# Hybrid attention and recurrent layer on one core: the down projection of the ConvFFN as 2x2 blocks with seven products

## The chip, the cores and the metric

One core of a Trainium2 chip runs the whole program in one launch. The metric is the device time of that launch in microseconds, the median of several runs; lower is better. Five engines work side by side: TensorE (PE, the matrix products), VectorE (DVE), ScalarE (ACT), GpSimd (POOL) and SyncE (SP, which here issues nearly all transfers in one in-order queue). Products land in PSUM, which has eight banks; everything else stands in SBUF or in DRAM.

## The reference, cut to what matters

2048 prompt tokens and 64 sample tokens pass one layer: attention and a gated recurrence (the "mixers"), then the ConvFFN. Only the ConvFFN's end is changed.

```python
h = modulate(x, norm_ffn_g[l], shift, scale)
up, cf_new = causal_dwconv(h @ ffn_up_w[l], cf_prev, ffn_conv_w[l], ffn_conv_b[l])
val, gt = jnp.split(up, 2, axis=-1)                                   # 2 x 2816 channels
x = x + gate[:, None, :] * ((val * jax.nn.gelu(gt)) @ ffn_down_w[l])  # 2816 -> 1024: the down projection
y = rmsnorm(x, final_norm_g)
```

All arrays are float32. The kernel keeps that precision by splitting every matrix factor into two float16 halves, a high one (the value cast) and a low one (value minus high), and adding three products (high by high, high by low, low by high) for each one wanted.

## The kernel before, in words

Columns are the 2112 tokens, kept as two halves of 1056 (TH) and worked on 352 (CF) at a time. Channels are tiles of 128: 8 tiles (KT) of the model width, 22 (NF) of the hidden width.

**Up rounds.** Round f makes one value tile and one gate tile of the hidden layer. The up projection is done as 2x2 blocks with seven products (Strassen-Winograd): 7 products x 3 column blocks x 4 k-tiles x 3 passes = 252 matmuls of 352 columns. Beside it, for the tile pair of round f-1, ACT and DVE run the convolution (`first_tap`, `ffn_conv`: four DVE instructions over 2114 columns), the GeLU and the product of value and gate (`product`), and split the weights of round f+1 (`up_hi` on ACT, `up_lo` on DVE). The gated tile is split into halves too (`product_hi`, `product_lo`) and stored to DRAM (`store_hidden`).

**Down projection, before.** The eight row tiles of the down weights are loaded and split whole (`down_hi`, `down_lo`, 2816 columns each) during and after the last round. Then six column blocks c follow each other: for each of them 8 row tiles m x 22 k-tiles x 3 passes = 528 matmuls, with the hidden halves read from DRAM in one large transfer per block (`hidden`). All 3168 matmuls run through the helper `passes` (L2545), as do the products of the other stages. For each row tile DVE adds the residual (`y_new`, L2413), ACT squares it (L1628), DVE sums the squares (`add_square`), and once for each block PE sums them over the partitions (`sum_squares2`, L2767), ACT takes the root (L1620), DVE inverts it (`inverse`, L2431) and scales the tile (`finish`, L2438), and SP stores y.

**What sets the order.** Nothing is scheduled: each engine's program is written out by hand and runs in that order, and semaphores hold an instruction until what it needs is there. `pe.wait_ge(g_ev, ...)` keeps PE from a bank until DVE has emptied it.

## Time and profile before

| what | value |
|---|---|
| three timed runs | 2755.87 (median), 2757.07, 2752.3 us |
| span of the profiled execution, first to last instruction | 2749.8 us |
| so outside the span, against the median | 6.1 us |
| PE busy in the span | 2703.3 us, 98% |
| DVE, ACT, POOL busy | 1606.0 us (58%), 1301.4 us (47%), 306.4 us (11%) |
| up rounds 1 to 21 | about 1491 to 2258 us |
| down projection on PE | 2258 to 2736 us |

The profiled execution's own time is not among the three listed; its span is what the trace gives, and the time around it is taken as the difference above. A busy share of PE counts pipelined matmuls, so it says that PE has no gaps, not that it works at its peak.

### The profile page before, as it was taken

How to read it: one execution, taken by the hardware profiler on the slowest of the kernel's cores; microseconds unless marked ns; L12 is line 12 of the kernel's file. 1: busy time of each engine (PE TensorE's matmuls, PEld its weight loads, DVE VectorE, ACT ScalarE, POOL GpSimd, SP SyncE). 2: the span in 40 equal slices, each digit the busy share in tenths (PEclk: the TensorE clock that was granted, in tenths of full speed). 3: DMA queues.
4: the chain of work that ended last, by engine and by line, in shares of the span. 5: the costliest groups of instructions: out<-in, count | busy, mean ns of one | idle time of the engine just before them, and what ended most of it. 6: DMA issues, size and time to landing. Idle time of an engine off the chain costs nothing.

```text
span 2749.8 us, 49269 instructions
## 1 busy us (share of the span) xinstructions
PE 2703.3 (98%) x19058; PEld 1816.5 (66%) x19058; DVE 1606.0 (58%) x3110; ACT 1301.4 (47%) x2497; POOL 306.4 (11%) x295
## 2 busy tenths in 40 slices
PE   7999999999999999999999999999999999999998
PEld 2456666666678886559986666666666666666665
DVE  5966473746556665777787677766677663211112
ACT  4966474746566664124566445445445452211111
POOL 2600000000037896000000000000000000000000
PEclk9999999999999999999999999999999999999999
DMA  8622122121474541556641111111111165223211
GB/s 283 208 91 90 70 76 103 64 71 69 128 194 112 127 188 59 217 209 164 158 113 50 59 62 62 46 62 47 62 62 62 46 209 165 84 88 98 90 43 43
DMA packets 214342, 291.11 MB, mean 106 GB/s; under 512 B 58704, under 2 KB 163664, under 8 KB 209312
## 3 DMA queue, kind: packets, MB, share of 16 engines
q1 hardware_dynamic: 204256, 277.44, 31.8%
q10 hardware_dynamic: 8848, 8.74, 0.9%
q8 instruction: 112, 1.84, 0.3%
q0 software_dynamic: 1072, 2.65, 0.3%
q14 instruction: 54, 0.44, 0.1%
HBM read 201.96 MB, written 89.46 MB: 106 GB/s over the span
## 4 chain that ended last, share of the span: by engine, by line
PE 86%; ACT 4%; DVE 4%; DMA 3%; issue 2%; POOL 1%; SPq 0%; DVEq 0%; ACTq 0%; POOLq 0%
PE ps L2545 74%; PE ps L2637 4%; PE ps L2624 3%; PE ps L2613 2%; DMA arena<-in_w_mod_rest 2%; PE ps L2469 1%; PE ps L2651 1%; ACT arena L1288 1%; POOL arena L889 1%; PE ps L2586 1%; DVE arena L2038 1%; DVE arena L2116 1%; ACT arena L1003 1%; ACT arena L1295 1%; DMA arena<-in_w_proj 1%
## 5 line engine op out<-in xcount | busy, mean ns | idle before, releaser
L2545 PE MATMUL ps<-arena 128*128 128x352 f16 (+1 forms) x15048 | 2086.3, 300 | 5.8 <-DVE arena L2237 1.7
L2545 PEld LDWEIGHTS ps<-arena 128*128 128x128 f16 x15048 | 1410.7, 97 | 677.0 <-issue 3.4
L2413 DVE SCALAR_TENSOR_TENSOR arena<-ps,arena 128x352 f32<-128x352 f32 (+1 forms) x64 | 30.0, 490 | 353.6 <-PE ps L2545 353.6
L1446 ACT ACTIVATE arena<-ps 128x352 f32<-128x352 f32 x264 | 119.8, 464 | 190.9 <-PE ps L2545 190.9
L1628 ACT ACTIVATE arena<-arena 128x352 f32<-128x352 f32 x48 | 23.8, 496 | 377.5 <-DVE arena L2413 377.5
L2651 PE MATMUL ps<-arena 128*128 128x424 f16 (+1 forms) x960 | 173.5, 342 | 2.0 <-DVE arena L2116 1.4
L2237 DVE SCALAR_TENSOR_TENSOR arena<-arena 128x512 f16<-128x512 f32 x154 | 103.8, 689 | 120.2 <-ACT arena L1410 120.2
L2637 PE MATMUL ps<-arena 128*128 128x64 f32 (+2 forms) x1200 | 150.6, 271 | 0.5 <-DVE arena L2080 0.5
L2651 PEld LDWEIGHTS ps<-arena 128*128 128x128 f16 x960 | 92.5, 97 | 82.7 <-issue 2.4
L2637 PEld LDWEIGHTS ps<-arena 128*128 128x128 f32 (+2 forms) x1200 | 144.2, 192 | 3.1 <-issue 1.4
L1483 ACT ACTIVATE arena<-arena 128x2114 f32<-128x2114 f32 x44 | 94.6, 2149 | 101.8 <-DVE arena L2292 96.6
L1086 ACT ACTIVATE arena<-ps 128x352 f32<-128x352 f32 x192 | 80.8, 463 | 120.5 <-PE ps L2545 120.5
L2305 DVE SCALAR_TENSOR_TENSOR arena<-arena 128x2114 f32<-128x2114 f32 x44 | 106.4, 2418 | 52.3 <-ACT arena L1483 52.3
L1295 ACT ACTIVATE arena<-ps 128x512 f32<-128x512 f32 (+3 forms) x136 | 76.3, 561 | 102.5 <-PE ps L2624 102.4
L935 POOL TENSOR_TENSOR arena<-arena 128x1024 f32<-128x1024 f32 (+6 forms) x147 | 118.6, 807 | 13.8 <-POOL arena L928 3.9
L1804 DVE SCALAR_TENSOR_TENSOR arena<-arena 128x512 f16<-128x512 f32 x112 | 73.9, 687 | 64.2 <-ACT arena L1065 64.1
L2309 DVE SCALAR_TENSOR_TENSOR arena<-arena 128x2114 f32<-128x2114 f32 x44 | 106.5, 2420 | 0.4
L1288 ACT ACTIVATE arena<-arena 128x640 f32<-128x640 f32 (+5 forms) x136 | 102.8, 756 | 3.4 <-DVE arena L2059 3.2
L2059 DVE CUSTOM_DVE_ANT_0 arena<-ps,arena 128x640 f32<-128x640 f32 (+5 forms) x136 | 100.2, 737 | 0.3 <-issue 0.2
L2514 PE MATMUL ps<-arena 128*128 128x512 f16 (+1 forms) x408 | 91.6, 383 | 7.3 <-DVE arena L1734 5.3
L2624 PE MATMUL ps<-arena 128*128 128x128 f32 (+1 forms) x600 | 92.9, 281 | 5.1 <-ACT arena L1288 2.9
L1410 ACT ACTIVATE arena<-arena 128x512 f16<-128x512 f32 x154 | 93.3, 624 | 0.0
(213 smaller groups left out, 2598.2 us busy)
## 6 DMA issues: line engine op xcount, KB each, us to landing
arena<-in_w_up SPq DMA_DIRECT2D x44, 512.0 KB, 3.9
ffn_hidden<-arena SPq DMA_DIRECT2D x44, 512.0 KB, 3.3
arena<-ffn_hidden SPq DMA_DIRECT2D x5, 3872.0 KB, 16.1
arena<-gates SPq DMA_DIRECT2D x8, 2112.0 KB, 9.6
arena<-in_w_proj SPq DMA_DIRECT2D x32, 512.0 KB, 4.5
gates<-arena SPq DMA_DIRECT2D x16, 1024.0 KB, 7.6
arena<-in_w_mod_rest SPq DMA_DIRECT2D x32, 512.0 KB, 4.0
arena<-in_w_down SPq DMA_DIRECT2D x7, 1408.0 KB, 6.2
```

Of the source, the lines that this page charges most:

```text
L935: pool.tensor_tensor(out, djunk[:, :, 0:w], djunk[:, :, w:2 * w], ALU.add).then_inc(ada_step, 1)
L1288: act.activation(pr[0:x.rows, x.h, 0:x.w], pr[0:x.rows, x.h, 0:x.w], ACT.Exp, scale=-1.0, bias=least[0:x.rows, x.h:x.h + 1], accum_out=sm[ ...
L1295: act.activation(pt[:, x.h, 0:m * P], ps[:, 4, 0:m * P], ACT.Copy).then_inc(t_act, 1)
L1446: act.activation(fcp[(0, 1, 2, 0)[i]][q], ps[:, bank_of((0, 2, 3, 4)[i], q), 0:CF], ACT.Copy, scale=CSF)\
L2059: dve.tensor_tensor_reduce(pr[0:rows, h, 0:w], src, bias[x.b][0:rows, h, x.b0:x.b0 + w], 1.0, 3.0e38, ALU.add, ALU.min, least[0:rows, h:h ...
L2237: dve.scalar_tensor_tensor(fsp[:, c, :, 1, :], src.rearrange("p (k m) -> p k m", k=4), -WSF if c == 6 else WSF, fsp[:, c, :, 0, :], ALU.mu ...
L2305: dve.scalar_tensor_tensor(out, u[:, 1:1 + LF], tap(1), out, ALU.mult, ALU.add).then_inc(f_conv, 1)
L2309: dve.scalar_tensor_tensor(out, u[:, 2:2 + LF], tap(2), out, ALU.mult, ALU.add).then_inc(f_conv, 1)
L2545: mm = pe.matmul(out, wt[:, k, wp, :], act_t[:, k, hp], start=(first and k == 0 and n == 0), stop=(last and k == K - 1 and n == 2), skip_g ...
L2624: mm = pe.transpose(ps[0:k, 4 + c // 4, (c % 4) * P:(c % 4) * P + x.rows], pr[0:x.rows, x.h, c * P:c * P + k], ident[0:x.rows, 0:x.rows])
L2637: mm = pe.matmul(ps[0:x.rows, 6, 64 * x.h:64 * x.h + 64], pt[0:k, x.h, c * P:c * P + x.rows], vv[x.b][0:k, x.v0 + c, 64 * x.h:64 * x.h + 6 ...
L2651: mm = pe.matmul(out, wt[:, wp, k, :], mixT[:, k, hp, t:t + w], start=(k == k0 and m == 0), stop=(k == k1 - 1 and m == 2))
```

## The change: what it does

The down projection takes the same form as the up projection: 2x2 blocks with seven products. A block row of the weights is a pair of row tiles, a block of the inner dimension a pair of k-tiles, and the two column blocks of a product are the same 352 columns of the two token halves. So there are three groups of columns (NG), four pairs of row tiles in each, twelve steps n in all (ND), and 11 pairs of k-tiles (NI). A step has 7 products x 11 x 3 = 231 matmuls.

- The gated tile is no longer split in the up rounds (`product_hi`, `product_lo` go); SP stores it in float32.
- The sums of weight blocks are made beside the up rounds in 44 units, two in each of rounds 1 to 16 and three in each of rounds 17 to 20: SP loads a unit (256 KB), POOL forms four sums of 128x128, ACT and DVE split seven tiles into halves (`unit_hi`, `unit_lo`), SP stores them (448 KB) to DRAM. The down projection reads them from there (`weight_load`).
- For each of the three groups the 11 bases (the four blocks of gated tiles of a k-pair, 704 KB) are loaded (`base_load`), POOL forms four sums of 128x352 (`base_sums`), ACT casts three blocks and four sums (`base_hi`, 1056 and 1408 columns), DVE subtracts (`base_lo`). The float32 blocks have two stage buffers (and one more for the very first group's last base); the halves stand in one set `dact[0..10]`, shared by all groups.
- A step is cut into chunks of bases, (0,4), (4,8), (8,11): all seven products of a chunk run before the next chunk. The first step takes bases 0 to 3 together and then one at a time. The last step is one chunk.
- The seven products of a step are combined by DVE in eleven small instructions over 352 columns (two copies from PSUM by ACT).
- The sums of squares of a whole group (8 row tiles x 2 halves, 16 tiles of 352 columns) are taken on PE inside the first step of the next group.

```diff
+            def base_load(s):
+                g, i = s // NI, s % NI
...
+                    to, done = stage[s % 2], b_loaded[s % 2]
+                    if s >= 2:
+                        sp.wait_ge(b_lo, 2 * (s - 1))
+                sp.dma_start(to.rearrange("p b t -> p (b t)"),
+                             hid_d[:, g, 2 * i:2 * i + 2].rearrange("p k h t -> p (k h t)")).then_inc(done, 16)
...
+            def base_sums(s):
+                b12, b11, b22, b21 = (stage_of(s)[:, k] for k in range(4))
...
+                if s >= 2:
+                    pool.wait_ge(b_lo, 2 * (s - 1))
...
+                pool.tensor_tensor(t0, b12, b11, ALU.subtract).then_inc(b_sum, 1)
+                pool.tensor_tensor(t1, b22, b12, ALU.subtract).then_inc(b_sum, 1)
+                pool.wait_ge(b_sum, 4 * s + 1)
+                pool.tensor_tensor(t2, b22, t0, ALU.subtract).then_inc(b_sum, 1)
+                pool.wait_ge(b_sum, 4 * s + 3)
+                pool.tensor_tensor(t3, b21, t2, ALU.subtract).then_inc(b_sum, 1)
...
+            def base_hi(s):
...
+                    act.wait_ge(q_filled, pair_used(4 * g - 1, i))
+                act.activation(dact[i][:, 0:3, 0], stage_of(s)[:, 1:4], ACT.Copy).then_inc(b_hi, 1)
+                act.wait_ge(b_sum, 4 * s + 4)
+                act.activation(dact[i][:, 3:7, 0], dsum[s % 2], ACT.Copy).then_inc(b_hi, 1)
...
+            def base_lo(s):
+                i = s % NI
+                dve.wait_ge(b_hi, 2 * s + 1)
+                dve.tensor_tensor(dact[i][:, 0:3, 1], stage_of(s)[:, 1:4], dact[i][:, 0:3, 0], ALU.subtract).then_inc(b_lo, 1)
+                dve.wait_ge(b_hi, 2 * s + 2)
+                dve.tensor_tensor(dact[i][:, 3:7, 1], dsum[s % 2], dact[i][:, 3:7, 0], ALU.subtract).then_inc(b_lo, 1)
...
+            for n in range(ND - 1):
+                g, s = n // 4, NI * (n // 4 + 1)
+                if n % 4 == 3:
+                    for k in range(5):
+                        base_lo(s + k)
+                top_left(n)
+                if n % 4 == 3:
+                    base_lo(s + 5)
+                upper_sum(n)
...
+                add_square(n, 3)
+                if n % 4 == 3:
+                    base_lo(s + 6)
+                    base_lo(s + 7)
+                    for h in range(2):
+                        inverse(g, h)
+                    for k in range(4):
+                        finish(g, k)
+                        if k < 3:
+                            base_lo(s + 8 + k)
...
+            def sum_squares2(g, h):
+                if g < NG - 1:
+                    pe.wait_ge(g_acc, 16 * g + 16)
...
+            for n in range(ND):
+                for x in range(len(chunks_of(n))):
+                    for k in range(7):
+                        down_product(n, x, k)
+                        if n in (4, 8) and x == 0 and k in (1, 3):
+                            sum_squares2(n // 4 - 1, k // 2)
```

The order of instructions, with what each waits for, shows the three places of which the prediction speaks. The first is DVE at the end of a group of columns. Before, a block of columns ended like this (L2413 adds the residual, L2424 and L2427 sum the squares, L2431 inverts, L2438 scales):

```order
L2413 SCALAR_TENSOR_TENSOR arena<-ps,arena 128x352 [waits res_loaded1,g_filled]
L2427 TENSOR_TENSOR arena<-arena 128x352 [waits g_acc,norm_sq]
L2413 SCALAR_TENSOR_TENSOR arena<-ps,arena 128x352 [waits g_filled]
L2424 COPY arena<-arena 128x352 [waits norm_ss,norm_sq]
L2413 SCALAR_TENSOR_TENSOR arena<-ps,arena 128x352 [waits g_filled]
L2427 TENSOR_TENSOR arena<-arena 128x352 [waits g_acc,norm_sq]
L2431 RECIPROCAL arena<-arena 128x352 [waits norm_std]
```

Nothing but the work on finished tiles stood there. In the changed kernel the same place, the fourth step of a group, reads (L2584 and L2586 are `base_lo` of the next group's bases; the first two rows are the last of five such pairs, the fifth and sixth row are a sixth pair; L2687 and L2679 are the first product's combination and residual; L2733 is `add_square`):

```order
L2584 TENSOR_TENSOR arena<-arena 128x3x352 [waits b_hi]
L2586 TENSOR_TENSOR arena<-arena 128x4x352 [waits b_hi]
L2687 TENSOR_TENSOR arena<-ps,arena 128x352 [waits q_cp,q_ev,q_filled]
L2679 SCALAR_TENSOR_TENSOR arena<-arena 128x352 [waits kc_loaded,q_ev]
L2584 TENSOR_TENSOR arena<-arena 128x3x352 [waits b_hi]
L2586 TENSOR_TENSOR arena<-arena 128x4x352 [waits b_hi]
L2695 TENSOR_TENSOR arena<-ps,arena 128x352 [waits q_cp,q_ev,q_filled]
L2733 TENSOR_TENSOR arena<-arena 128x352 [waits g_acc,norm_sq]
L2701 TENSOR_TENSOR arena<-ps,arena 128x352 [waits q_cp,q_ev,q_filled]
L2703 TENSOR_TENSOR arena<-arena 128x352 [waits q_ev]
L2679 SCALAR_TENSOR_TENSOR arena<-arena 128x352 [waits q_ev]
```

What moved: twelve instructions that wait for ACT, POOL and loads of the next group now stand ahead of most of the work on the group that ends. The second place is PE at that point. Before, the column sum of squares stood between two row tiles (L2767):

```order
L2545 MATMUL ps<-arena 128x352 [waits g_ev]
L2545 MATMUL ps<-arena 128x352 x65
L2767 MATMUL ps<-arena 128x352 [waits norm_std,g_acc]
L2545 MATMUL ps<-arena 128x352 [waits g_ev]
L2545 MATMUL ps<-arena 128x352 x65
```

In the changed kernel the fifth step begins so (L3131 are the products, L3095 the sums of squares):

```order
L3131 MATMUL ps<-arena 128x352 [waits b_lo]
L3131 MATMUL ps<-arena 128x352 x2
L3131 MATMUL ps<-arena 128x352 [waits q_cp]
L3131 MATMUL ps<-arena 128x352 x11
L3095 MATMUL ps<-arena 128x352 [waits g_acc]
L3131 MATMUL ps<-arena 128x352 [waits q_ev]
L3131 MATMUL ps<-arena 128x352 x11
L3131 MATMUL ps<-arena 128x352 [waits q_ev]
L3131 MATMUL ps<-arena 128x352 x11
L3095 MATMUL ps<-arena 128x352 [waits norm_std,g_acc]
```

The sum of squares now stands 24 matmuls behind the end of the step whose squares it adds, where it stood 132 behind. The third place is SP's queue behind the last up round. Before (L807 loads hidden halves, L796 and L797 store the last tile, L841 loads residuals):

```order
L796 DMA ffn_hidden<-arena 128x2x1024 [waits f_plo]
L797 DMA ffn_hidden<-arena 128x2x32
L796 DMA ffn_hidden<-arena 128x2x1024
L797 DMA ffn_hidden<-arena 128x2x32
L807 DMA arena<-ffn_hidden 128x2x352 [waits hb_last,h_stored]
L841 DMA arena<-x_after_mixers 128x8x352 [waits x1_stored1,x1_stored0]
L841 DMA arena<-x_after_mixers 128x8x352
```

And in the changed kernel (L896, L898 and L900 store the last tile, here its second half; L950 loads weight combinations, L961 residuals, L937 the bases 8, 10 and 9):

```order
L896 DMA ffn_hidden<-arena 128x2x352
L898 DMA ffn_hidden<-arena 128x320
L900 DMA ffn_hidden<-arena 128x32
L950 DMA arena<-down_combinations 128x1792
L961 DMA arena<-x_after_mixers 128x2x352 [waits f_conv,x1_stored1,x1_stored0]
L961 DMA arena<-x_after_mixers 128x2x352 x3
L937 DMA arena<-ffn_hidden 128x1408 [waits b_lo,h_stored]
L937 DMA arena<-ffn_hidden 128x1408 [waits h_stored]
L937 DMA arena<-ffn_hidden 128x1408 [waits b_lo,h_stored]
```

One small load followed the last store before; now three base loads do, with a weight load and four residual loads ahead of them.

## Rows read from the trace of the kernel before

**Rows 1.** The page: busy time, and PE's clock in 40 slices.
```profile
PE 2703.3 (98%) x19058; PEld 1816.5 (66%) x19058; DVE 1606.0 (58%) x3110; ACT 1301.4 (47%) x2497; POOL 306.4 (11%) x295
...
PEclk9999999999999999999999999999999999999999
```

**Rows 2.** Stretches: start and end, length, busy us by engine, clock, DMA.
```profile
1491.00:2253.00 762.00, 762.00 (x5110) 494.04 (x5109) 525.12 (x669) 375.59 (x629) 0.00 (x0) 1.00 0.19 66
2400.00:2500.00 100.00, 100.00 (x667) 65.16 (x666) 16.79 (x32) 11.33 (x21) 0.00 (x0) 1.00 0.29 91
2240.00:2250.00 10.00, 10.00 (x69) 6.49 (x68) 3.94 (x8) 4.39 (x9) 0.00 (x0) 1.00 1.09 382
```

**Rows 3.** PE's waits from 2200 us on: total, times, longest us.
```profile
PE ps L2767 <- DVE arena L2427: 1.9, 1, 1.9
PE ps L2545 <- DVE arena L2413: 1.2, 1, 1.2
```

**Rows 4.** GpSimd's instructions by shape: count, busy us, mean ns.
```profile
L935 POOL TENSOR_TENSOR arena<-arena 128x512 f32<-128x512 f32 x21 | 26.8, 1278 | 1.6
L935 POOL TENSOR_TENSOR arena<-arena 128x256 f32<-128x256 f32 x21 | 15.4, 733 | 1.6
L935 POOL TENSOR_TENSOR arena<-arena 128x128 f32<-128x128 f32 x21 | 9.7, 461 | 1.6
```

**Rows 5.** DVE and ACT from 2216 us on, by shape.
```profile
L2427 DVE TENSOR_TENSOR arena<-arena 128x352 f32<-128x352 f32 x42 | 21.8, 518 | 0.3 <-ACT arena L1628 0.2
L2431 DVE RECIPROCAL arena<-arena 128x352 f32<-128x352 f32 x6 | 14.1, 2348 | 1.5 <-ACT arena L1620 1.5
L2438 DVE TENSOR_TENSOR arena<-arena 128x1760 f32<-128x1760 f32 x6 | 11.9, 1988 | 0.0
L2309 DVE SCALAR_TENSOR_TENSOR arena<-arena 128x2114 f32<-128x2114 f32 x4 | 9.7, 2417 | 0.0
L2438 DVE TENSOR_TENSOR arena<-arena 128x1056 f32<-128x1056 f32 x6 | 7.5, 1253 | 0.0
...
L1628 ACT ACTIVATE arena<-arena 128x352 f32<-128x352 f32 x48 | 23.8, 496 | 377.5 <-DVE arena L2413 377.5
L1513 ACT ACTIVATE arena<-arena 128x2816 f16<-128x2816 f32 x7 | 17.8, 2545 | 10.3 <-DVE arena L2328 9.7 <-DVE arena L2323 0.6
...
L1495 ACT ACTIVATE arena<-arena 128x1057 f16<-128x1057 f32 x4 | 4.1, 1079 | 5.4 <-DVE arena L2313 5.4
```

**Rows 6.** Transfers: count, KB each, median us from issue to landing.
```profile
arena<-in_w_up SPq DMA_DIRECT2D x44, 512.0 KB, 3.9
...
arena<-in_w_down SPq DMA_DIRECT2D x1, 1024.0 KB, 4.9
```

**Rows 7.** Timeline of the last up round, ACT: its first product's third block.
```profile
2225.79 0.47 ACT L1446 ACTIVATE arena<-ps 128x352 f32<-128x352 f32 x1 [1.06 <-PE ps L2545]
```

**Rows 8.** Timeline of DVE and ACT at the end of an up round.
```profile
2030.20 2.42 DVE L2305 SCALAR_TENSOR_TENSOR arena<-arena 128x2114 f32<-128x2114 f32 x1 [2.51 <-ACT arena L1483]
...
2027.87 2.15 ACT L1483 ACTIVATE arena<-arena 128x2114 f32<-128x2114 f32 x1 [5.08 <-DVE arena L2292]
```

**Rows 9.** Timeline of GpSimd and DVE early in the kernel, one instruction each.
```profile
54.96 0.45 POOL L889 TENSOR_SCALAR arena<-arena 128x128 f32<-128x128 f32 x1 [4.46 <-DVE arena L1718]
56.73 1.92 POOL L889 TENSOR_SCALAR arena<-arena 128x128 f32<-128x128 f32 x1
57.21 0.68 DVE L1747 TENSOR_TENSOR arena<-arena 128x512 f32<-128x512 f32 x1
57.81 0.68 DVE L1749 TENSOR_TENSOR arena<-arena 128x512 f32<-128x512 f32 x1
```

**Rows 10.** PE's longest early gap, and stretches behind it as in rows 2.
```profile
59.88 12.08 PE L2514 MATMUL ps<-arena 128*128 128x512 f16 x48 [2.72 <-DVE arena L1734]
...
60.00:62.00 2.00, 2.00 (x6) 0.62 (x6) 1.11 (x2) 0.26 (x2) 1.87 (x3) 0.50 0.00 0
62.00:64.00 2.00, 2.00 (x8) 0.83 (x7) 1.43 (x2) 2.00 (x5) 0.00 (x0) 0.74 0.08 27
```

More of the change, by code:

```diff
@@ L46 @@
 NX, NP = 6, 9
+NI, NG = NF // 2, 3
 COLS = {}
@@ L216, in build, with stage_of @@
+        gsq = [at_(o, CF) for o in (36320, 41422)]
+        gacc = [at_(o, CF) for o in (41984, 42336)]
+        first_cp, fourth_cp, upper, whole = (at_(o, CF) for o in (43904, 44256, 44608, 51136))
+        def stage_of(s):
+            return stage_last if s == NI - 1 else stage[s % 2]
         bias_d = nc.dram_tensor("bias_rows", (8, 768), F32, kind="Internal").ap()
@@ new lines, in root2 @@
+            def root2(g, h):
+                act.wait_ge(norm_ss, 2 * NE + 2 * g + h + 1)
+                act.activation(gacc[h], ps[:, norm_bank(g, h), 0:CF], ACT.Sqrt, scale=1.0 / D, bias=epsc).then_inc(norm_std, 1)
+            for n in range(ND):
+                g, last = n // 4, n % 4 == 3 and n < ND - 1
+                s = NI * (g + 1)
+                if last:
+                    for k in range(5):
+                        base_hi(s + k)
+                first_copy(n)
+                if last:
+                    base_hi(s + 5)
+                fourth_copy(n)
+                for k in range(4):
+                    square2(n, k)
+                    if n == ND - 1 and k == 2:
+                        root2(g, 0)
+                if last:
+                    base_hi(s + 6)
+                    base_hi(s + 7)
+                    for h in range(2):
+                        root2(g, h)
+                    for k in range(8, NI):
+                        base_hi(s + k)
@@ L2375, in ffn_round @@
                 product(f - 1)
-                if not tile_is(f, NF - 1):
-                    dve.wait_ge(p_lo, 7 * NR + 7 * f + 7)
-                    weight_sums(f + 1)
-                product_lo(f - 1)
+                if tile_is(f, LAST):
+                    base_lo(0)
+                    base_lo(1)
+                    for q in range(3):
+                        block(f, 2, q)
+                        block(f, 1, q)
+                    base_lo(2)
+                    return
+                units = wu_units(f, late)
+                dve.wait_ge(p_lo, 7 * NR + 7 * f + 7)
+                weight_sums(f + 1)
+                unit_lo(units[0])
                 for c in range(5):
-                    if tile_is(f, NF - 1):
-                        down0_lo(c)
-                    else:
-                        up_lo(f + 1, c)
+                    up_lo(f + 1, c)
+                    if late and c == 2:
+                        unit_lo(units[1])
                 for q in range(3):
@@ L2387, in ffn_round @@
                     block(f, 1, q)
[L2388 to L2392 removed]
+                unit_lo(units[-1])
+            with nc.vector.Fori(1, W_LATE) as f:
                 ffn_round(f)
[L2394 to L2401 removed]
@@ L2417, in add_square, with bank_of_product @@
-            def add_square(c, m):
-                u = 8 * c + m
+            with nc.vector.Fori(W_LATE, LAST) as f:
+                ffn_round(f, True)
+            ffn_round(LAST)
+            base_lo(3)
+            ffn_conv(LAST, 0)
+            base_lo(4)
+            ffn_conv(LAST, 1)
+            base_lo(5)
+            product(LAST)
+            for s in range(6, NI):
+                base_lo(s)
+            def bank_of_product(n, c):
+                return ps[:, down_bank(n, products_of(n).index(c)), 0:CF]
@@ L2453, in _ @@
+            upper_sum(ND - 1)
+            top_right(ND - 1)
+            bottom_right(ND - 1)
+            for k in range(2):
+                add_square(ND - 1, k)
+            top_left(ND - 1)
+            add_square(ND - 1, 2)
+            inverse(NG - 1, 0)
+            finish_half(0, 0)
+            bottom_left(ND - 1)
+            add_square(ND - 1, 3)
+            finish_half(0, 1)
+            inverse(NG - 1, 1)
             for i in range(2):
-                finish(5, i)
+                finish_half(1, i)
```

676 lines of the change are left out of this document (433 added, 243 removed).

## The prediction

> **What bounds the kernel now.** The page comes first: PE is busy for 2703.3 of 2749.8 us and its clock is granted whole in every slice, so only PE's own work, or new gaps in it, can move the time [rows 1]. The stretches give the pace: the up rounds and the down projection run PE without a break, the down projection with 667 matmuls in 100 us, 0.150 us each, while DVE works 17 us of that 100, ACT 11 and GpSimd none [rows 2]. PE's list of waits from 2200 us on holds 1.2 us for a bank and 1.9 us at the very end; the hand-over from up to down costs nothing [rows 3]. The reader should see two things: an engine with nothing to hide behind, and three others that are nearly idle in the last 480 us. The change takes work from the first and gives it to the others, at moments when PE waits for them.
>
> **What is removed.** Twelve steps of 231 matmuls are 2772 where 3168 stood: 396 x 0.150 = 59.4 us less on PE. That is counted, not hoped for. The bank wait of 1.2 us goes too.
>
> **The up rounds: no cost.** In a round of 37.6 us DVE works 525/762 of the time [rows 2], some 26 us. `product_lo`, 2114 columns, goes; two or three `unit_lo` of 384 and 512 columns come, about 1.2 us each, a difference of at most 1.3 us. At the round's end DVE waits 2.5 us for `first_tap` and ACT 5.1 us for DVE [rows 8], and behind that lies the work of one round ahead. GpSimd gets 8 to 12 sums of 128 columns at 0.46 us [rows 4]. The cover is this slack: were it gone, twenty rounds would pay a microsecond or more each.
>
> **The price of a base.** Four steps in a loop, since a stage buffer is loaded again only when its base is split, and there are two:
> - load, 704 KB: between 512 KB in 3.9 and 1024 KB in 4.9 us [rows 6], 4.2 us
> - four GpSimd sums of 352 columns: between 0.73 (256) and 1.28 us (512) [rows 4], so 0.94 each and, two of them waiting for one before, 4.15 us
> - ACT's second cast, 1408 columns: between 1.08 and 2.55 us [rows 5], 1.4 us (the first, 1.1 us, lies beside the sums)
> - DVE's second subtraction, 1408 columns, by 1.25 us for 1056 [rows 5], 1.6 us
>
> That is 11.4 us for two bases, 5.7 us each, where PE eats a base in 21 x 0.150 = 3.15 us. So supply is slower than demand whenever both run at once: at the start of the first group and at the change of groups.
>
> **First step.** The third block of the last round's first product was done at 2225.8 [rows 7], 36 matmuls into the round, so PE ends the up rounds at 2225.8 - 5.4 + 37.6 = 2258.0 = E. Base 4 is loaded once base 2 is split, E-2, and is split itself at about E+9.3. ACT's order puts its second cast ahead of the last tile's `first_tap` (2.15 us [rows 8]), so that ends at E+11.2; two convolution steps of 2.42 us, GeLU 2.1 us [rows 5], base 5's subtractions and the product bring the last hidden tile to E+21.4. Base 6 is split at E+24.3 and base 7 at E+30.3. Behind the tile SP issues six stores, one weight load and four residual loads, 3.0 MB, ahead of base 8; at 382 GB/s, the best stretch [rows 2], that is 7.8 us, so base 8 lands at E+33 and bases 10 and 9 at E+35 and E+37. Sums at 4.15 us each then give base 10's halves at E+48.7, and PE's 21 matmuls end at E+51.8. Without waits the step ends at E+34.6: 17 us lost. I take 20, for the contention below; the ends are 12 and 24.
>
> **Two changes of group.** Count from the start of a group's fourth step. PE's chunks end at 12.6, 25.2 and 34.6 us. Halves of the next group may be written from 12.6 on; bases 1 and 2 of it are split at 16.6 and 19.5, and two loops later, at 43.3, base 6. On DVE base 5 and base 6 stand ahead of most of the step's combinations. Behind base 6 come nine small combinations, four additions of squares at 0.52 us and one square on ACT at 0.50 [rows 5]: 7 us, so the group's last square is in at 50.3. But PE wants it after two products of the next step, at 34.6 + 3.6 = 38.2, for `sum_squares2`. PE idles 12.1 us. The second sum waits for a root that stands behind base 8's casts on ACT (1.9 us), and base 11, behind two reciprocals of 2.35 us and three `finish` [rows 5], comes 1.5 us late: 15.5 us for each change. That is the lower bound; it needs no contention at all.
>
> **Contention.** GpSimd and DVE disturb each other in this trace. An instruction of 0.45 us alone takes 1.92 us when DVE runs additions with two SBUF inputs back to back, and those keep their 0.68 us [rows 9]. In the new loop a pair of bases asks 8 x 0.94 us of GpSimd and 2 x 2.9 us of DVE, 13.3 us if they exclude each other, and up to 15 when each waits for the other's end. Base 6 then comes at 48 to 52 us, the last square at 55 to 60, and with the later bases the change of group costs 22 to 28 us. I take 24, nearer the low end, because part of an instruction's time is its start.
>
> The Trainium skill, "SBUF — State Buffer", section Who interferes with whom, says that a DVE instruction with two SBUF inputs contends with a GpSimd instruction that reads SBUF, and that whoever issues first holds the pair for the whole instruction. By that rule the upper figures hold, about +30 us in all; were it not so, the lower, about -11 us. Rows 9 show GpSimd's half of it, no row here shows DVE held by a long GpSimd instruction.
>
> **Clock.** After gaps of which the longest was 2.7 us, PE ran at half its clock, 1.2 for 2.4 GHz, for some 3 us [rows 10]. The waits above are longer, and each of the three places may pay 1 to 2 us: 3 us, ends 0 and 8.
>
> **The end.** The last base product is combined by one instruction more (0.5 us), and `inverse` and `finish` of the first half (2.35 and 1.99 us [rows 5]) must fit into the last product's 33 matmuls; by my count they end 1.7 us late: +2.2 us.
>
> **The sum.** -59.4 - 1.2 + 20 + 2 x 24 + 3 + 2.2 = +12.6 us. The profiled span of 2749.8 becomes 2762.4; the median lies 6.1 us above the span, so 2768.5.
>
> **Rivals.**
> - *The same loop without contention* (faster). Terms: 17 + 31 + 0 + 1.7 against 60.6, or -10.9 us, 2745; with 12 for the first step 2740. For it: DVE's additions were hardly touched [rows 9], and reading phases may interleave. Against it: GpSimd is on the loop's path, and it was held fourfold. It decides from a change of group below some 18 us. Chance 0.20.
> - *Light contention*, 19 us for each change and 19 us at the start: -60.6 + 19 + 38 + 2 + 2.2 = +0.6 us, no change that can be measured. Chance 0.17.
> - *The up rounds stall as well* (slower by much): ACT waits in its order for GpSimd's unit sums, which DVE's 2.42 us instructions hold up, and copies that PE needs stand behind. A microsecond in each of twenty rounds makes 2788. Against it: the sums have some 10 us from load to use in a round, and the lists of waits show no PE wait in the rounds. Chance 0.08.
> - *The forecast*, contended changes of group: 2768, own range 2758 to 2786. Chance 0.55.
>
> That the saving doesn't come I exclude: the matmuls are counted.
>
> **The numbers.** What a measurement of this kernel can tell from no change is about 0.2%, 5.5 us. Faster holds the first rival and the edge of the second, 0.22; same the rest of the second, 0.15; slower the forecast and the third rival, 0.63. The range runs from the uncontended case to the contended upper bound of -60.6 + 24 + 56 + 8 + 2.2 = +29.6 us with the first rival's low corner left out: 2742 to 2788.
>
> **What the profile would show.** Matmuls of L3131 at 0.150 us: the saving. A PE wait of 12 to 22 us at each of the two first `sum_squares2` (L3095) on DVE's addition of squares: the change of group; under 8 us there says the order of DVE's queue doesn't matter. Waits for `base_lo` in the first step that sum to 12 to 24 us. GpSimd sums of 352 columns at 0.94 us each say no contention, 1.3 us and more says contention, and DVE's `base_lo` above 1.25 and 1.6 us that it goes both ways. PE gaps before 2220 us would make the third rival. Wrong would be the forecast above all if the loop for two bases took under 11 us, or if PE found the squares ready.

## The result and the profile after

The changed kernel, C from here on, takes 2794.89 us (median of 4 runs, 2789.84 to 2797.45) where the kernel before, B, takes 2754.09 (4 runs beside them, 2750.55 to 2757.07): ratio 1.0146, 95% interval 1.0131 to 1.0160, or 41 us slower. The direction was forecast, the size was not: 2768 was said, with a range that ended at 2788.

The page of the changed kernel, PE's busy line, its slices and the granted clock; in [rows 1] the clock is whole in every slice.

```profile
span 2794.9 us, 50241 instructions
PE 2674.5 (96%) x18662; PEld 1786.5 (64%) x18662; DVE 1761.8 (63%) x3321; ACT 1367.9 (49%) x2618; POOL 580.9 (21%) x603
PE   7999999999999999999999999999999988879797
PEclk9999999999999999999999999999999999989898
```

Two stretches of it by windows: the up rounds, and the middle of the down projection (busy and instructions of each engine, clock, DMA).

```profile
1491.00:2253.00 762.00, 762.00 (x5111) 494.00 (x5109) 540.73 (x734) 383.35 (x680) 113.30 (x187) 1.00 0.29 103
2540.00:2600.00 60.00, 60.00 (x402) 38.91 (x401) 19.84 (x22) 13.29 (x17) 17.46 (x16) 1.00 0.38 135
```

The up rounds are as full as in [rows 2] although DVE, ACT, GpSimd and DMA do more. Between the changes of group PE is full as well, 402 matmuls in 60 us, 0.149 each. So the loss lies at the down projection's start and at its two changes of group. PE's timeline shows it: start, duration, line, count, and in brackets the idle time ahead with its releaser. L3131 is the down projection, L3095 `sum_squares2`, L2586 the second subtraction of `base_lo`, L2733 `add_square`, L1849 `first_copy`, L1666 `c21`, ACT's copy of the last up round's product out of PSUM.

```profile
2264.03 7.36 PE L3131 MATMUL ps<-arena 128*128 128x352 f16 x48
2275.57 11.45 PE L3131 MATMUL ps<-arena 128*128 128x352 f16 x57 [4.19 <-ACT arena L1666]
2288.50 3.32 PE L3131 MATMUL ps<-arena 128*128 128x352 f16 x21 [1.48 <-DVE arena L2586]
2294.95 4.92 PE L3131 MATMUL ps<-arena 128*128 128x352 f16 x21 [3.13 <-DVE arena L2586]
2301.71 3.32 PE L3131 MATMUL ps<-arena 128*128 128x352 f16 x21 [1.84 <-DVE arena L2586]
2312.77 9.36 PE L3131 MATMUL ps<-arena 128*128 128x352 f16 x42 [7.74 <-DVE arena L2586]
2324.15 108.53 PE L3131 MATMUL ps<-arena 128*128 128x352 f16 x723 [2.02 <-DVE arena L2586]
2433.25 0.62 PE L3131 MATMUL ps<-arena 128*128 128x352 f16 x3 [0.57 <-DVE arena L2586]
2438.69 3.39 PE L3131 MATMUL ps<-arena 128*128 128x352 f16 x12 [4.82 <-ACT arena L1849]
2456.95 1.54 PE L3095 MATMUL ps<-arena 128*128 128x352 f32 x2 [14.87 <-DVE arena L2733]
2458.28 5.63 PE L3131 MATMUL ps<-arena 128*128 128x352 f16 x24
2463.76 0.75 PE L3095 MATMUL ps<-arena 128*128 128x352 f32 x2
2464.35 19.05 PE L3131 MATMUL ps<-arena 128*128 128x352 f16 x126
2488.32 116.62 PE L3131 MATMUL ps<-arena 128*128 128x352 f16 x762 [4.93 <-DVE arena L2586]
2610.65 3.70 PE L3131 MATMUL ps<-arena 128*128 128x352 f16 x12 [5.71 <-ACT arena L1849]
2627.31 1.54 PE L3095 MATMUL ps<-arena 128*128 128x352 f32 x2 [12.96 <-DVE arena L2733]
...
2658.90 83.78 PE L3131 MATMUL ps<-arena 128*128 128x352 f16 x543 [4.99 <-DVE arena L2586]
2745.01 27.93 PE L3131 MATMUL ps<-arena 128*128 128x352 f16 x174 [2.34 <-DMA arena<-down_combinations]
...
2773.37 5.11 PE L3131 MATMUL ps<-arena 128*128 128x352 f16 x33
...
```

Bases are counted from 0 from here on, as in the code; the prediction's paragraph on the changes of group counts them from 1.

What the reader is to see: the up rounds end at 2264.0, the first step has gaps of 20.4 us, the first change of group (2431 to 2499) gaps of 25.2, and the second 23.7. Those sums are almost what was forecast. But a gap isn't a loss. Matmuls behind a longer gap run slower: 21 take 4.92 us at 2294.95 and 3.32 at 2301.71, 24 take 5.63 us and, in the middle of a group, 3.6. The window behind the wait for squares has its clock at 0.50, 1.2 for 2.4 GHz, after 14.87 us in which PE did nothing:

```profile
2456.00:2462.00 6.00, 5.05 (x15) 2.61 (x16) 5.53 (x6) 5.98 (x6) 0.00 (x0) 0.50 0.15 23
```

What each place costs is the time over its matmuls at 0.150 us:

- first step: the last 21 matmuls start at 2324.15 and end at 2327.3; 231 at full pace from 2264.0 would end at 2298.6: **28.7 us** lost, 20 forecast
- first change: the fourth step ends at 2324.15 + 714 x 0.150 = 2431.3. Its successor has 57 matmuls left at 2488.32, which take 8.5 us and 2.3 more at a lowered clock, so it ends at 2499.1: 67.8 us for 34.6 us of matmuls, **33.2** lost, 24 forecast
- second change, in the same way (eighth step's end 2603.1, 57 matmuls in 8.5 and 2.5 us from 2658.90): **32.2**, 24 forecast
- the weights' wait at 2745.01 with the slower matmuls behind it (174 in 27.93 for 26.05 us): **4.2**, not forecast
- the end, from the last L3131 at 2778.5: 16.4 us for 13.6, **2.8**, 2.2 forecast.

That is 101.1 us against the 59.4 and 1.2 saved, +40.5. The up rounds ended 6.0 us later than in the profile before (2264.0 for 2258.0, see the last experiment), which makes 46.5 where the two spans differ by 45.1; the rest is the rounding of these counts. The medians differ by 40.8, since C's profiled execution took 2797.01 us, 2 above its median, and B's was one of its faster ones (see the end of the account of the prediction).

### The profile page after: what moved, and what is told of

It reads as the page before. It is cut to its first block and busy times, and to the rows that moved or that the text cites. A ratio compares the mean times of both kernels' runs of the same rounds, so it can differ in the third digit from the quotient of the medians.

```text
span 2794.9 us, 50241 instructions
## 1 busy us (share of the span) xinstructions
PE 2674.5 (96%) x18662; PEld 1786.5 (64%) x18662; DVE 1761.8 (63%) x3321; ACT 1367.9 (49%) x2618; POOL 580.9 (21%) x603
## 5 line engine op out<-in xcount | busy, mean ns | idle before, releaser
L2886 PE MATMUL ps<-arena 128*128 128x352 f16 (+1 forms) x11880 | 1611.4, 297 | 4.6 <-DVE arena L2495 1.7
L2886 PEld LDWEIGHTS ps<-arena 128*128 128x128 f16 x11880 | 1101.3, 97 | 510.2 <-DVE arena L2062 2.3
L3131 PE MATMUL ps<-arena 128*128 128x352 f16 x2772 | 438.9, 322 | 43.8 <-DVE arena L2586 26.7
L3131 PEld LDWEIGHTS ps<-arena 128*128 128x128 f16 x2772 | 275.8, 100 | 207.5 <-DVE arena L2586 21.9
L1120 POOL TENSOR_TENSOR arena<-arena 128x128 f32<-128x128 f32 x44 | 22.8, 519 | 1038.9 <-DMA arena<-in_w_down 1038.9
L2992 PEld LDWEIGHTS ps<-arena 128*128 128x128 f16 x960 | 92.5, 97 | 82.6 <-issue 2.3
L2687 DVE TENSOR_TENSOR arena<-ps,arena 128x352 f32<-128x352 f32 x12 | 6.3, 523 | 151.8 <-PE ps L3131 150.5
```

Source lines behind the costliest of these rows:

```text
L2886: mm = pe.matmul(out, wt[:, k, wp, :], act_t[:, k, hp], start=(first and k == 0 and n == 0), stop=(last and k == K - 1 and n == 2), skip_g ...
L2992: mm = pe.matmul(out, wt[:, wp, k, :], mixT[:, k, hp, t:t + w], start=(k == k0 and m == 0), stop=(k == k1 - 1 and m == 2))
L3131: mm = pe.matmul(ps[:, down_bank(n, k), 0:CF], dwt(i)[:, wi, wp, :], dact[i][:, bi, hp, :], start=(i == 0 and m == 0), stop=(i == NI - 1 a ...
```

## The experiments

Every run was timed beside B on the same chip. In the last two columns a negative sign is faster than B.

| run | median us | B beside it | ratio, 95% interval | to B, us |
|---|---|---|---|---|
| C | 2794.89 | 2754.09 | 1.0146 (1.0131, 1.0160) | +40.8 |
| e1_filled | 2789.62 | 2752.95 | 1.0129 (1.0107, 1.0151) | +36.7 |
| e2_later_sums | 2806.97 | 2752.95 | 1.0190 (1.0167, 1.0213) | +54.0 |
| e3_evac_first | 2793.61 | 2752.95 | 1.0144 (1.0125, 1.0163) | +40.7 |
| e4_no_new_bases | 2731.24 | 2752.95 | 0.9918 (0.9897, 0.9940) | -21.7 |
| e5_sums_on_dve | 2783.44 | 2755.32 | 1.0108 (1.0093, 1.0122) | +28.1 |
| e6_early_slots | 2772.48 | 2755.32 | 1.0067 (1.0052, 1.0083) | +17.2 |
| e7_order_gpsimd | 2769.93 | 2755.32 | 1.0059 (1.0043, 1.0075) | +14.6 |
| e8_order_dve | 2767.59 | 2755.32 | 1.0046 (1.0030, 1.0061) | +12.3 |
| e9_first_step | 2794.63 | 2753.20 | 1.0156 (1.0143, 1.0169) | +41.4 |
| e10_all_orders | 2740.91 | 2753.20 | 0.9957 (0.9943, 0.9971) | -12.3 |
| e11_sizes_alone | 2753.65 | 2753.20 | 1.0002 (0.9991, 1.0012) | +0.5 |
| e12_first_on_dve | 2730.61 | 2756.45 | 0.9895 (0.9875, 0.9915) | -25.8 |

### Is it the clock? (e1)

My first reading of the profile was that the gaps are as forecast, so the halved clock, for which I had 3 us, must be the error: some 24 us of slower matmuls. The test keeps PE at work while it waits.

```
+    if n in (4, 8) and x == 0 and k == 1:
+        pe.wait_ge(q_ev, ev(n - 1, "c11"))
+        for r in range(84):
+            pe.matmul(ps[:, down_bank(n, 2), 0:CF], dwt(r % 4)[:, 0, 0, :], dact[r % 4][:, 0, 0, :], start=True, stop=True, ...)
     if n in (4, 8) and x == 0 and k in (1, 3):
         sum_squares2(n // 4 - 1, k // 2)
```

> The changed kernel with PE kept at work while it waits at the two changes of group: 84 more matmuls (12.6 us at 0.150) before the first sum of squares, which had waited 14.87 and 12.96 us, and 50 more (7.5 us) would be needed for the later wait for a base, which is left empty here. Every wait for DVE and ACT stays as it was. If the halved clock after a gap is what my sum had too small, the sum of squares and the 24 matmuls behind it run at full clock (0.75 for 1.54 us and 3.6 for 5.63 us): 3 us less for each change. As the next base comes no earlier, the wait of 4.9 us for it grows by these 3 us, so the total stays at 2790 to 2795. If the slow matmuls had another cause, they stay at 1.54 and 5.6 us. If the 84 don't fit into the wait, the total rises.

PE's timeline at its first change of group; L3142 are the added matmuls.

```profile
2441.32 13.59 PE L3142 MATMUL ps<-arena 128*128 128x352 f16 x84
2454.90 0.86 PE L3095 MATMUL ps<-arena 128*128 128x352 f32 x2
2455.60 3.76 PE L3131 MATMUL ps<-arena 128*128 128x352 f16 x24
...
2486.24 116.19 PE L3131 MATMUL ps<-arena 128*128 128x352 f16 x759 [5.83 <-DVE arena L2586]
```

The clock is back (3.76 for 5.63 us, 0.86 for 1.54), and the next wait grows from 4.93 to 5.83, at the second change from 4.99 to 7.20. The down projection as a whole is 0.8 us shorter in the profile; by the medians the run is 4.1 us nearer to B than C is, with intervals of 4 us up and down on C's distance and 6 on this one's, so a gain is not shown. The run gave full clock only to the matmuls at the squares, some 3 of the 7 us by which matmuls are slow at each change. For the rest C's rows decide: its last base is ready when PE goes on at 2488.32, and even at full clock PE would need 8.5 us for the 57 matmuls behind it. So the bases alone make 30.9 of the 33.2 us, and 29.7 of the 32.2 at the second change. Slow matmuls ahead of such a wait take time that PE would wait anyway; only those behind the last wait cost, 2.3 and 2.5 us. My first reading fell: what was short in the forecast was the supply of bases.

### Where does the supply hang? (e2, e3, e4)

e2 moves the two sums of squares one chunk later on PE.

```
-    if n in (4, 8) and x == 0 and k in (1, 3):
+    if n in (4, 8) and x == 1 and k in (1, 3):
```

> The sums of squares of the last group stand one chunk (84 matmuls, 12.6 us) later in PE's program, nothing else. Theory of two delays (squares late and bases late): the waits of 14.87 and 12.96 us are gone, but PE reaches the second chunk some 13 us ahead of base 7 and waits 10 to 13 us there for base_lo; 7 us won for each change, 2781 in all. Rival, that the place of the sums alone costs the time: both waits go and none takes their place, 28 us won, 2767. Rival, that bases alone set the pace: nothing won, 2793 and more.

PE's timeline in e2, at the last pairs of the same step:

```profile
2482.11 1.06 PE L3131 MATMUL ps<-arena 128*128 128x352 f16 x3 [3.61 <-DVE arena L2586]
2491.35 116.50 PE L3131 MATMUL ps<-arena 128*128 128x352 f16 x759 [8.18 <-DVE arena L2586]
```

The theory and the first rival forecast a gain, and the second rival no change; by the distances to B the run is 13 us slower than C. The waits of 14.87 and 12.96 us did go. But on DVE bases 8 to 10 stand behind the reciprocals, these behind ACT's roots, and these behind PE's sums. A later sum on PE makes the last bases later, and PE waits for them: 2491.35, where C goes on at 2488.32 although its up rounds ended 2.8 us later.

e3 puts combinations and squares of the fourth step ahead of bases 4 and 5 on ACT and DVE; DVE's part of the edit, cut:

```
-    for k in range(5):
+    for k in range(4):
         base_lo(s + k)
     top_left(n)
-    if n % 4 == 3:
-        base_lo(s + 5)
     upper_sum(n)
     add_square(n, 0)
+    if n % 4 == 3:
+        base_lo(s + 4)
```

> On DVE and ACT the combinations and squares of a group's fourth step stand ahead of bases 4 and 5 of the next group instead of behind them; PE's program is unchanged. If the order of DVE's queue makes the squares late, PE's wait of 14.87 and 12.96 us falls to under 3 us, the 4.8 and 5.7 us for the first copy fall to under 3, and PE waits some 10 us for base 7 at the second chunk instead of 5: 12 us won for each change, 2771. If contention of GpSimd and DVE makes everything late whatever the order, less than 5 us is won for each: 2785 or more.

The same place in e3, where L3098 is `sum_squares2`, L3134 the down projection and L1868 the root:

```profile
2445.29 1.54 PE L3098 MATMUL ps<-arena 128*128 128x352 f32 x2 [12.53 <-DVE arena L2735]
...
2460.83 1.51 PE L3098 MATMUL ps<-arena 128*128 128x352 f32 x2 [9.21 <-ACT arena L1868]
...
2485.90 115.59 PE L3134 MATMUL ps<-arena 128*128 128x352 f16 x759 [2.72 <-DVE arena L2588]
```

The theory missed too: nothing won, as its rival had said. Counted from the end of the up rounds, the first sum of squares starts 8.6 us earlier than in C, and the first copy costs nothing. Then the second sum waits 9.2 us for a root that stands behind base 7's casts on ACT. PE gets its last base at 2485.90, 224.9 us after the end of its up rounds; in C that is 224.3 and in e1 223.8. The waits ahead can be moved about; the last base decides.

e4 leaves the new bases out, so that groups two and three are multiplied by the first group's halves: no `base_load`, `base_sums`, `base_hi` and `base_lo` from the 12th on.

> Left out: the bases of the second and third group of columns are neither loaded nor summed nor split, so these groups are multiplied by the first group's halves, and y of their columns is not the reference's. What stays of the change is the 2772 matmuls, the first step's loop and the tail. By my sum the second and third change of group cost 24 us each and their share of the halved clock 7 each, so 2795 - 49 - 14 - 2 = 2730, below the kernel before by some 20 us. If the halved clock comes from the first step alone, or the lost time lies elsewhere than at the changes of group, the time is over 2742.

PE's timeline in e4 from the end of the first step on:

```profile
2320.18 110.78 PE L3111 MATMUL ps<-arena 128*128 128x352 f16 x738 [2.20 <-DVE arena L2575]
...
2435.75 135.04 PE L3111 MATMUL ps<-arena 128*128 128x352 f16 x900
```

2731.24 for 2730 forecast. Both changes of group cost nothing here, and the squares, roots and reciprocals are done in time without the bases. So the bases carry all of the 62 us between this run and C (33.2 + 32.2 by the account above, which the intervals allow). What is left is B less 22 us, with the first step still at its full price.

### What makes a base slow? (e5, e6)

e5 moves the sums of groups two and three from GpSimd to DVE (`dve_sums(s)`, the same four instructions, ahead of `base_lo(s)`; GpSimd keeps the first 11).

> For the second and third group the four sums of 352 columns of each base stand on DVE ahead of its base_lo, GpSimd has none of them, so no GpSimd instruction can hold DVE. Theory, that contention makes the loop of two bases 13 us: DVE then needs 4 x 0.52 + 1.25 + 1.62 = 5.0 us for a base, 10 us for two, and the squares come up to 8 us earlier at each change of group: 2779 in all. Rival, that contention costs little and the sums were free on GpSimd: DVE's queue gets 2.1 us longer for each of eight bases, the squares come 5 to 15 us later: 2805 to 2825.

Groups by line and form in the first change: in C, two of the four GpSimd sums and DVE's two subtractions (count, busy us, mean ns):

```profile
L1149 POOL TENSOR_TENSOR arena<-arena 128x352 f32<-128x352 f32 x10 | 16.7, 1665 | 0.0
L1146 POOL TENSOR_TENSOR arena<-arena 128x352 f32<-128x352 f32 x11 | 11.1, 1010 | 104.6 <-DMA arena<-ffn_hidden 104.6
L2586 DVE TENSOR_TENSOR arena<-arena 128x1408 f16<-128x1408 f32 x10 | 19.0, 1900 | 11.3 <-ACT arena L1729 11.3
L2584 DVE TENSOR_TENSOR arena<-arena 128x1056 f16<-128x1056 f32 x10 | 17.4, 1743 | 12.0 <-ACT arena L1727 12.0
```

and in e5 the same two subtractions, with one of the sums on DVE:

```profile
L2601 DVE TENSOR_TENSOR arena<-arena 128x1408 f16<-128x1408 f32 x8 | 13.0, 1625 | 1.9 <-ACT arena L1729 1.9
L2599 DVE TENSOR_TENSOR arena<-arena 128x1056 f16<-128x1056 f32 x8 | 10.0, 1253 | 2.7 <-ACT arena L1727 2.7
L2587 DVE TENSOR_TENSOR arena<-arena 128x352 f32<-128x352 f32 x8 | 4.2, 520 | 5.7 <-DMA arena<-ffn_hidden 5.7
```

DVE took on 2.1 us for each base, and the kernel became 12.7 us faster by the distance to B (16 forecast). In C a base's two subtractions cost 3.64 us for 2.88, and its GpSimd sums 1.0 to 1.67 us each for 0.93. GpSimd and DVE disturb each other both ways. For DVE this is shown by the removal: without GpSimd the durations are back. For GpSimd C's rows show it, two sums of one form just before and just after DVE begins on base 0 at 2410.51:

```profile
2407.59 0.93 POOL L1149 TENSOR_TENSOR arena<-arena 128x352 f32<-128x352 f32 x1
2411.27 1.95 POOL L1149 TENSOR_TENSOR arena<-arena 128x352 f32<-128x352 f32 x1
```

But e5 took two things away at once. Undisturbed, the four sums of a base take 3.7 us on GpSimd (2405.81 to 2409.49) and 2.1 on DVE. Two bases took 12.1 to 14.6 us in C, would take 11.4 without contention by the prediction's price, and took 9.9 in e5. By these an estimate is that contention makes somewhat more than half of the gain and the slower GpSimd sum the rest; no run separates them.

e6 leaves sums and order alone and frees the slots earlier: the fourth step takes its pairs in smaller chunks, and the first two bases are loaded ahead.

```
+    if n in (3, 7):
+        return [(0, 1), (1, 2), (2, 4), (4, 6), (6, 8), (8, NI)]
     return [(0, NI)] if n == ND - 1 else [(0, 4), (4, 8), (8, NI)]
```

> The fourth step of groups one and two goes through its first eight pairs in chunks of 1, 1, 2, 2, 2 pairs instead of 4 and 4, so the first slot for new halves is free 3.2 us after its start and not 12.6, and the first two bases are loaded ahead of the step. Order of all other work unchanged. Theory, that the loop of bases runs at its own pace from the first free slot: everything at the change of group moves 9 us forward, the wait for squares falls from 15 and 13 to 4 to 6 us, 2776 in all. Rival, that the squares hang on the step's last chunk on PE and on the queue behind it: less than 3 us won for each change, 2789 and more.

2772.5 for 2776 forecast, 23.6 us nearer to B than C: some 12 us for each change, more than the 9 by which the first slot is free earlier. The wait for squares fell only to 10.2 and 10.4 us (4 to 6 forecast), but the first copies' waits of 4.8 and 5.7 went. PE has no cost from smaller chunks: 738 matmuls in 110.76 us.

### All orders together (e7, e8, e9, e10, e12)

e7 and e8 join early slots, e3's order, the sums of squares at the end of the next step's first chunk, and that step's later pairs in chunks of two and one; e7 with the sums on GpSimd, e8 on DVE.

> All changes of order together, sums on GpSimd as in the change: early slots, combinations and squares ahead of bases 4 and 5, the sums of squares at the end of the next step's first chunk, and that step's later pairs in chunks of two and one. If the loop of 13.2 us for two bases is all that is left, the last base is ready 6 + 11 x 6.6 = 79 us after the fourth step's start, where PE could end the next step's first seven products at 69: 8 to 10 us lost for each change instead of 24, and half of the clock's loss there gone: 2795 - 30 - 7 = 2758. If another chain (root, reciprocal, finish, store, residual) takes over: over 2775.

> As the run before, but with the sums of the second and third group on DVE. DVE then has 11 x 5.0 us of bases, some 9 of combinations and squares, 4.7 of reciprocals and 5.4 of finish, 74 us from 5 us after the fourth step's start: again some 8 to 10 us lost for each change, 2758, if both counts are right. If contention is dearer than 1.6 us for a base, this one is the faster of the two by up to 10 us; if DVE's queue is the bound, it is the slower.

Both came out 10 to 12 us above what was said, and their difference of 2.3 us is within the intervals, so whether contention or DVE's queue weighs more with this order isn't told apart by them. e8's DVE does a base in 4.94 us, but sat idle for 4.7 us before the fourth step's first combination, with base 4 loaded and behind it in the queue; and PE waited 3.3 and 2.8 us for weights that SP asked for behind the stores of y.

e9 changes only the first step of C: on ACT `c21` and the second `first_tap` ahead of base 4's casts, on DVE both convolution steps in a row, on SP bases 8 to 10 ahead of the residuals.

> The changed kernel with another order in the first step alone: ACT evacuates the last round's three blocks and does the second first_tap ahead of base 4's second cast (instead of behind it, where it waited for GpSimd), DVE does both convolution steps in a row, and SP loads bases 8, 10 and 9 ahead of the residuals. My count: the wait of 4.2 us for c21 is gone, the last hidden tile is done some 8 us earlier, and the waits for bases 8 to 10 shrink by 6 us: the first step loses 12 instead of 20 us and some clock with it, 2783 to 2786 in all. If the loop of bases (load, GpSimd, ACT, DVE) sets the end whatever the order: over 2791.

The last wait of e9's first step, on PE; the up rounds end at 2261.00:

```profile
2318.21 110.94 PE L3131 MATMUL ps<-arena 128*128 128x352 f16 x726 [2.20 <-DVE arena L2586]
```

Missed: the rival holds (2794.63, over 2791). The wait for `c21` went, the last tile was done 21.1 us after the up rounds' end instead of 27.4, and the last base came at 57.2 instead of 60.1. The loop of bases, with GpSimd in it, gave back half of what the order had won, and of the other 3 us the median shows nothing.

e10 adds e9's order to e8, puts base 4 ahead of the combinations, the last three `finish` behind base 10, weights ahead of stores, and splits the last step's first two products so that the third lot of weights has twice the time.

> All orders together: that of the run before this, sums of groups two and three on DVE, early slots, base 4 ahead of the fourth step's combinations (DVE idled 5 us there), the finish of tiles 1 to 3 behind base 10, weights asked for ahead of the stores of y, and in the last step the first two products take their first eight pairs ahead of the last three (the weights' wait of 2.8 us). From the 2768 of e8: 8 to 10 us less in the first step, 4 to 5 for each change of group, 3 for weights, 3 to 4 in the last step: 2742 to 2746, below the kernel before. If the lost time only moves from one wait to the next: over 2757, no better than the kernel before.

2740.9, a little below the 2742 to 2746 said. e12 is e10 with the sums of bases 6 to 10 of the first group on DVE too:

```
-    for s in range(NI):
+    for s in range(6):
         base_sums(s)
-    if s >= NI:
+    if s >= 6:
         dve_sums(s)
```

> The run with all orders, and in the first step too the sums of the last five bases (7th to 11th) on DVE instead of GpSimd. In that run the last base of the first step was split 57.8 us after the end of the up rounds, with GpSimd sums of 0.93 to 2.3 us and base_lo stretched to 1.98 and 2.3 us beside them. Theory, that the exclusion of GpSimd and DVE sets the pace there as it did at the changes of group: DVE then needs 5 us for a base from about E+22 on, the last one is split at about E+49, 8 us earlier, 2733 in all. Rival, that loads, stores and the convolution steps of the last tile set the pace: under 3 us earlier, 2738 to 2743.

PE's timeline in e12, where L3153 is the down projection:

```profile
2262.24 12.76 PE L3153 MATMUL ps<-arena 128*128 128x352 f16 x84
...
2311.55 116.16 PE L3153 MATMUL ps<-arena 128*128 128x352 f16 x774 [1.62 <-DVE arena L2608]
```

The last base of the first step is ready 49.3 us after the up rounds' end (49 forecast), 57.8 in e10. The same move alone was worth 13.5 us by the distances to B, more than the 8 said; the trace shows 8.5 us by the last base and 1.7 by matmuls behind it that run slower in e10 (774 in 117.83 us for 116.16), and the rest is within the intervals. By the same distances e12 is 25.8 us faster than B and 67 faster than C, with the same 2772 matmuls.

### Is anything lost before the down projection? (e11)

> The kernel before with only the two sizes of the change: the arena of 55200 instead of 53200 columns and the DMA scratch of 8192. All profiles of changed kernels end the up rounds 3 to 6 us later than before, and show a wait of 2.3 to 2.6 us on DVE's scores near 1050 us where before has 1.1 us. If the sizes are the cause, this run shows it too, and is 3 us slower (ratio 1.001); if not, ratio 1.000 and the wait at 1.1 us. The difference is near what can be measured, so the profile decides.

The stretch around that wait by windows, in e11 (PE's busy time first, its clock third from the end):

```profile
1000.00:1100.00 100.00, 94.85 (x688) 73.38 (x687) 58.19 (x218) 49.64 (x117) 72.96 (x63) 0.94 0.32 121
```

B with the change's two sizes shows the same stretch as C (C: 95.21 busy, clock 0.94; B: 96.42, 0.98), in a profiled execution whose last up round came 7.1 us later than B's (the third copy at 2232.91, for 2225.79 in [rows 7]), and its median is B's. So the sizes cost nothing that the medians show (0.5 us, interval 3 up and down), and the 6 us by which C's profile entered the down projection late are of the size by which B's executions differ (2748 to 2764 us). But the expectation wanted the profile to decide, and the profile isn't as clear: all changed kernels' profiles and e11's show this stretch slower, with a wait for DVE of 2.2 to 2.7 us near 1050 us, and B's only profile shows 1.1. Whether the sizes or the choice of B's one profiled execution makes that difference stays open.

## Why the prediction was wrong, step by step

- **What is removed**: right. 2772 matmuls at 0.150 us, and e4 shows the saving with only the first step's and the last step's losses against it.
- **Up rounds at no cost**: right, 762.00 of 762 us busy. The third rival is out.
- **Price of a base**: load 4.1 us (4.2 said), GpSimd sum 0.93 alone (0.94), ACT 1.37 (1.4), DVE 1.62 (1.6). The loop of two took 12.1, 14.6, 13.2 and 14.2 us in C, up to base 5; 13.3 to 15 was said for contention. About right. The loads of C in the down projection (KB each, median us to landing):

```profile
arena<-ffn_hidden SPq DMA_DIRECT2D x29, 704.0 KB, 4.1
arena<-down_combinations SPq DMA_DIRECT2D x30, 448.0 KB, 4.9
```

- **First step**: the step that failed first. 20 was said, 28.7 measured, above the end of 24. The last tile was expected at E+21.4 and came at E+27.4, since I let contention touch only the bases: here two convolution steps took 3.10 us for 2.42 beside GpSimd, and ACT kept `c21` and the second `first_tap` behind a cast that waited for base 4's sums, which took 7.4 us (2266.32 to 2273.76) for the 4.15 said. The last base, said for E+48.7, came at E+60.1. e10 and e12 show where most of it hangs: in an order common to both, the last base comes at E+57.8 with its sums on GpSimd and at E+49.3 with them on DVE. How much of that is contention and how much the slower sum stays open, as in e5. C's row of the last tile's product, which ends it at E+27.4:

```profile
2288.37 3.08 DVE L2571 SCALAR_TENSOR_TENSOR arena<-arena 128x2114 f32<-128x2114 f32 x1
```

- **Changes of group**: the order of queues was read rightly up to the squares: base 5 (the prediction's base 6) was split 50.7 us after the fourth step's start (48 to 52 said), the last square was in at 60.3 (55 to 60). The error is behind them. I worked out the last five bases only for the loop without contention, where the last comes some 26 us after the squares, and for the other case added nothing. In C they took 31.3 us, the last came at 91.6, and with it the change cost 30.9 us, 33.2 with the slow matmuls behind it, where I took 24 from a range of 22 to 28. Part of the 31.3 is in base 10's four sums, which began beside DVE's work at 2479.08 and took 6.1 us for the 4.15 said. And within the range I leaned to the low end, "because part of an instruction's time is its start". [rows 4] have such a part, some 0.19 us of each GpSimd sum, but no row said that DVE may work in it. C's rows for base 5, the last square and the last base:

```profile
2445.24 2.10 DVE L2586 TENSOR_TENSOR arena<-arena 128x1408 f16<-128x1408 f32 x1 [2.23 <-ACT arena L1729]
...
2455.02 1.87 DVE L2733 TENSOR_TENSOR arena<-arena 128x352 f32<-128x352 f32 x2
...
2486.64 1.62 DVE L2586 TENSOR_TENSOR arena<-arena 128x1408 f16<-128x1408 f32 x1 [2.23 <-ACT arena L1729]
```

- **Clock**: 3 us, ends 0 and 8. The slower matmuls sum to over 20 us, but only those behind the last wait of a place cost: none in the first step (21 in 3.3 us), 2.3 and 2.5 us at the changes, 1.9 at the last step's weights, 6.7 in all. That lies inside the ends, at twice the number taken. The prediction gave 1 to 2 us to each place without asking what follows the slow matmuls, so its nearness is in part luck.
- **The end**: +2.8 for 2.2. Right.
- **Not forecast**: 4.2 us for the last step's weights. A lot of weights is asked for when the step before has used the last, and PE wants it after 24 matmuls, 3.6 us later, while such loads take 4.9.
- **Base of the sum**: the 6.1 us between profiled span and median weren't time outside the span; that is 1.8 us in B's other executions (2753.20 for a span of 2751.4). The profiled execution was one of the faster. This changed no term. The range's upper end is a slip as well: +29.6 us makes 2785.5, and the 2788 given is the third rival's figure.

The account: 71 us was said for start, changes and clock together, 94.1 came (28.7, 60.6 and 4.8; 98.3 with the weights). So the direction came from the right mechanism, a supply of bases slower than PE's demand. What failed is the size of two terms, 20 for 28.7 in the first step and 24 for 30.9 and 29.7 at the changes: the first let contention touch only the bases and not the last tile's work ahead of them, the second priced the last five bases without it. The rivals that took contention for light are refuted. By the Trainium skill, "SBUF — State Buffer", section Who interferes with whom, a DVE instruction with two SBUF inputs and a GpSimd instruction that reads SBUF contend for a shared port pair that only one of them holds at a time. The rows of C agree in both directions (1.90 for 1.62 us on DVE, 1.67 for 0.93 on GpSimd), where the prediction's rows of B had shown only GpSimd's side.

## What to carry to other kernels

- A saving on the bound engine is worth what the supply behind it leaves. Take the new work out in one run (e4) to see the saving bare, then price the supply to its last piece, and for the contended case as carefully as for the clean one: PE waits for the last base, whatever stands ahead of it.
- Idle GpSimd time is not free for sums of SBUF tiles when DVE has two-input work in the same loop: four instructions more on DVE for each base made the kernel faster by 13 us, twice (e5, e12). With e7's order the same move gave 2.3 us, within the intervals.
- Where slots come free in lots, make the consumer's last round finer grained; this cost PE nothing and gave 24 us (e6). And move a wait only after asking what stands behind the instruction that it releases (e2).

## What the runs showed of the hardware that was not expected

In C a DVE instruction beside GpSimd sums grows by up to 0.73 us and by no more, whether it is short or long (0.79 was the most in e1 and e6). Three of C's rows, in the first change:

```profile
2460.07 1.25 DVE L2584 TENSOR_TENSOR arena<-arena 128x1056 f16<-128x1056 f32 x1
2470.14 1.98 DVE L2584 TENSOR_TENSOR arena<-arena 128x1056 f16<-128x1056 f32 x1
2472.05 2.35 DVE L2586 TENSOR_TENSOR arena<-arena 128x1408 f16<-128x1408 f32 x1
```

1.25 becomes 1.98 us and 1.62 becomes 2.35; an addition of squares of 0.52 us becomes 1.25, and a convolution step of 2.42 becomes 3.10. The surcharge doesn't grow with the instruction, and is somewhat less than a GpSimd sum of 0.93. That would fit a wait for the end of one GpSimd instruction rather than a shared rate; it was not tested by itself.
